# Second feed-forward, first product: seven Strassen-Winograd block products per pair of hidden tiles in place of eight, with the squared rows kept in DRAM

## The reference

```python
def rms_norm(x, gain):
    y = x * lax.rsqrt(jnp.mean(x * x, axis=-1, keepdims=True) + EPS)
    return y * gain

def sq_relu_mlp(h, w1, w2):            # w1: 1024 x 4096, w2: 4096 x 1024
    return jnp.square(jax.nn.relu(h @ w1)) @ w2
...
        h = h + sq_relu_mlp(rms_norm(h, mlp_norm_gain[layer]), mlp_w1[layer], mlp_w2[layer])
    return rms_norm(h, final_norm_gain)[:, N_META:]
```

## Time and profile before

| | us |
|---|---|
| median of three runs | 2773.19 (2771.89 to 2775.13) |
| the profiled execution | 2769.4, span 2767.6 |
| second feed-forward within it | 2028.55 to 2746.76 |

### The profile page before, as it was taken

One profiled execution on the slowest core, in us unless ns is written; L12 is line 12 of the kernel. 1 busy time (PEld: TensorE's weight loads), 2 busy tenths in 40 slices (PEclk: granted clock), 3 DMA queues, 4 the chain that ended last, 5 costly groups with the idle time before them and its releaser, 6 DMA issues.

```text
span 2767.6 us, 43631 instructions
## 1 busy us (share of the span) xinstructions
PE 2692.9 (97%) x18459; PEld 2423.2 (88%) x18459; DVE 1328.1 (48%) x1552; ACT 752.3 (27%) x1177; POOL 925.8 (33%) x403
## 2 busy tenths in 40 slices
PE   7998999999999999999999999999989999999998
PEld 7897998999999999999888888887768888888887
DVE  5387887442222322235677777779353222222234
ACT  3116886120100010002344344444221000110003
POOL 3130001344433443344323232324334444444441
PEclk9999999999999999999999999999999999999999
DMA  4110000111111111113111111112111111111111
GB/s 158 31 31 8 0 0 15 47 39 46 46 47 47 48 45 46 53 46 107 33 39 32 39 32 39 32 38 91 42 33 52 46 46 46 52 45 45 46 52 70
DMA packets 178141, 125.49 MB, mean 45 GB/s; under 512 B 4818, under 2 KB 171044, under 8 KB 177990
## 3 DMA queue, kind: packets, MB, share of 16 engines
q1 hardware_dynamic: 176694, 118.47, 14.0%
q10 hardware_dynamic: 1296, 4.73, 0.4%
HBM read 114.80 MB, written 8.39 MB: 45 GB/s over the span
## 4 chain that ended last, share of the span: by engine, by line
PE 84%; DVE 9%; issue 4%; ACT 3%; DMA 0%; ACTq 0%; SPq 0%; DVEq 0%
PE ps L1337 74%; PE ps L1471 3%; PE ps L1596 2%; PE ps L1564 1%; DVE kk L1172 1%; ACT prob L618 1%; PE ps L1421 1%; PE ps L1634 1%; ACT kk L716 1%; DVE kk L1169 1%; DVE tmp L901 1%; DVE y L967 0%; PE ps L1609 0%; DVE ssq L893 0%; DVE amax L1008 0%
## 5 line engine op out<-in xcount | busy, mean ns | idle before, releaser
L1337 PE MATMUL ps<-xh,wsp 128*128 128x512 f32 (+2 forms) x4864 | 1122.5, 355 | 13.8 <-POOL wsp L497 6.3
L495 POOL TENSOR_TENSOR wsp<-raw,ones 128x1024 fp32r<-128x1024 f32 x198 | 383.5, 1937 | 1784.8 <-PE ps L1337 1749.7
L1337 PEld LDWEIGHTS ps<-xh,wsp 128*128 128x128 f32 x4864 | 840.5, 189 | 100.3 <-issue 15.3
L1337 PE MATMUL ps<-xl,wsp 128*128 128x348 f32 (+2 forms) x2432 | 617.7, 351 | 0.0
L1337 PE MATMUL ps<-ah,wsp 128*128 128x348 f32 (+2 forms) x2560 | 567.0, 350 | 0.0
L497 POOL TENSOR_TENSOR wsp<-raw,wsp 128x1024 fp32r<-128x1024 f32 x198 | 533.5, 2694 | 15.5
L1337 PEld LDWEIGHTS ps<-ah,wsp 128*128 128x128 f32 x2560 | 443.1, 188 | 44.7
L1337 PEld LDWEIGHTS ps<-xl,wsp 128*128 128x128 f32 x2432 | 430.9, 189 | 44.3
L666 ACT ACTIVATE tmp<-tmp 128x1044 f32<-128x1044 f32 (+1 forms) x64 | 68.5, 1071 | 1096.1 <-DVE tmp L1070 555.6
L1337 PE MATMUL ps<-al,wsp 128*128 128x348 f32 (+1 forms) x1280 | 322.5, 349 | 0.0
L1337 PEld LDWEIGHTS ps<-al,wsp 128*128 128x128 f32 x1280 | 225.2, 188 | 23.2
(11 more groups left out here) (212 smaller groups left out, 2688.0 us busy)
## 6 DMA issues: line engine op xcount, KB each, us to landing
raw<-in_w SPq DMA_DIRECT2D x128, 512.0 KB, 3.7
raw<-in_c_w_in SPq DMA_DIRECT2D x40, 512.0 KB, 3.8
raw<-in_ab_w_in SPq DMA_DIRECT2D x12, 512.0 KB, 3.7
xst<-in_x SPq DMA_DIRECT2D x8, 512.0 KB, 6.6
raw<-in_ab_w_out SPq DMA_DIRECT2D x8, 512.0 KB, 3.5
h_kept<-h ACTq DMA_DIRECT2D x8, 512.0 KB, 2.6
h<-h_kept SPq DMA_DIRECT2D x8, 512.0 KB, 5.8
out<-ost SPq DMA_DIRECT2D x16, 256.0 KB, 3.0
```

What stands on the lines that cost most here:

```text
L495: nc.gpsimd.tensor_tensor(wsp[:, slot, 0, :], raw[:, slot, :], one, ALU.mult).then_inc(w_high, 1)
L1337: ins = M(ps[:, 3 * s + c, 0:n], w(a, k), b(k)[:, c0:c0 + n], start=(k == first and a == 0 and b is xa), stop=(k == last and a == 1))
```

## The change

Only the second feed-forward changes. Its first product is cut in blocks. Two hidden tiles (256 columns of w1) are a pair, `PAIRS` = 16. The inner width 1024 is halved, and so are the tokens. That is a 2 x 2 by 2 x 2 block product. `product(p, s, ...)` makes one of seven block products of pair p by the Strassen-Winograd scheme, 12 matmuls of 512 columns into one bank. So a pair takes 84 matmuls where two tiles took 96.

- **Weights.** GpSimd makes four sums of weight blocks per pair (`add` into `sw0` to `sw2`) and seven low parts (`low`), all of 512 columns. ScalarE makes the seven high parts (`high`, by a copy), each at most four products ahead (`wop` has four slots). In pairs 0 and 1 GpSimd makes these too.
- **Tokens.** At the start VectorE and ScalarE make four sums of token blocks (`ts`, `t3s`), each with high and low part for four row tiles. One replaces a quarter of `xh` and `xl`, the others are `t2h`, `t3h`, `t4h` and their low parts.
- **Results.** VectorE makes seven additions of 512 columns per pair, each from a bank and SBUF, then four rectifying steps within SBUF (`relu_half`). ScalarE copies one bank (`copy_first`), squares the four halves and stores each to the DRAM tensor `hidden_rows` (`keep`).
- **Second product.** The order is now all 16 pairs, then all eight `down` chunks. SP reloads each hidden row tile into `tmp`, ScalarE rounds it (`hidden_high`), VectorE takes the low part (`hidden_low`). `hh` and `hl` have two buffers of four tiles. `wsp` and `wop` share memory.

The diff, cut to its core (names are as in the changed kernel):

```diff
+        def bank_of(g):
+            return (2, 5, 0, 1, 3, 4)[g % 6] if g < 14 else (0, 1, 3, 4, 2, 5, 6, 7)[(g - 14) % 8]
...
+            def pair_load(p, part, free, count):
+                v1 = w1[1].rearrange("(k p) n -> p k n", p=P)
+                sp.wait_ge(free, count)
+                nc.sync.sem_inc(c_sp, 1)
+                nc.sync.dma_start(k4(raw[:, part, :]), v1[:, CH * part:CH * (part + 1), 2 * P * p:2 * P * (p + 1)]).then_inc(t_land[part], 16)
+            for p in range(1, PAIRS):
+                pair_load(p, 0, t_add, 4 * p)
+                if p == 1:
+                    pair_load(p, 1, t_low, 7)
+                else:
+                    pair_load(p, 1, t_low, 7 * p - 3)
...
+            def hidden_load(t):
+                if t == 0:
+                    sp.wait_ge(n_rc, 12)
+                elif t == 1:
+                    sp.wait_ge(t_low, 7 * PAIRS)
+                else:
+                    sp.wait_ge(l_l, 32 + t - 1)
...
+            hidden_load(0)
+            down_load(0)
+            down_load(1)
+            hidden_load(1)
+            for t in range(2, CH):
+                hidden_load(t)
+            for i in range(2, 32):
+                down_load(i)
+                if i + 2 < 32:
+                    hidden_load(i + 2)
...
+            def high(g, a):
+                if g < 2:
+                    pool.wait_ge(w_used, U_MLP1 - 1)
+                elif g < 4:
+                    pool.wait_ge(z_ready, HG_LAST + KT)
+                else:
+                    pool.wait_ge(t_done, g - 3)
+                nc.gpsimd.tensor_tensor(operand(g, 0), a, one4, ALU.mult).then_inc(t_high, 1)
+            def low(g, a):
+                pool.wait_ge(t_high, g + 1)
+                nc.gpsimd.tensor_tensor(operand(g, 1), a, operand(g, 0), ALU.subtract).then_inc(t_low, 1)
+            high(2, weight(1, 0))
+            low(2, weight(1, 0))
+            add(sw0, sw1[:], weight(0, 0), ALU.subtract)
+            pool.wait_ge(t_add, 2)
+            pool.wait_ge(n_ssq, 21)
+            add(sw2, sw0[:], weight(1, 0), ALU.subtract)
+            pool.wait_ge(t_add, 3)
+            high(3, sw2[:])
+            low(3, sw2[:])
...
+                landed(p, 0)
+                low(g, weight(0, 0))
+                landed(p, 1)
+                pool.wait_ge(t_low, 7 * p - 1)
+                add(sw1, weight(0, 1), weight(1, 1), ALU.add)
...
+                low(g + 1, sw0[:])
...
+                    high(g + 2, weight(1, 0))
+                low(g + 2, weight(1, 0))
+                pool.wait_ge(t_low, 7 * p)
+                add(sw2, sw0[:], weight(1, 0), ALU.subtract)
+                if own:
+                    high(g + 3, weight(1, 1))
...
+            def down_split(i):
+                if i < 2:
+                    pool.wait_ge(t_done, 7 * PAIRS - (1 if i == 0 else 0))
+                split(U_MLP1 + i, i % 2, 8 * (U_MLP1 + i - i % 2) + 16)
...
+            for k in range(CH):
+                act.wait_ge(z_free, HG_LAST + k + 1)
+                A(quarter(xh, k, 0), quarter(h, k, 0), ACT.Copy, scale=gain[:, k:k + 1]).then_inc(n_hi, 1)
+                A(x12[:, k, :], quarter(h, k, 1), ACT.Copy, scale=gain[:, k:k + 1]).then_inc(x_12, 1)
+                square_row(k)
+            for i in range(CH):
+                sum_high(i, quarter(xh, i, 1), ts[:, i, :])
+                act.wait_ge(z_free, HG_LAST + CH + i + 1)
+                A(xh[:, CH + i, real], h[:, CH + i, real], ACT.Copy, scale=gain[:, CH + i:CH + i + 1]).then_inc(n_hi, 1)
+                square_row(CH + i)
+            def copy_first(p):
+                act.wait_ge(t_done, 7 * p + 1)
...
+                A(p1[:], product_bank(p, 0), ACT.Copy).then_inc(t_cp, 1)
+            def high(g, a, ready, count):
+                act.wait_ge(ready, count)
+                act.wait_ge(t_done, g - 3)
+                A(operand(g, 0), a, ACT.Copy).then_inc(t_high, 1)
+                act.wait_ge(t_sq, 4 * p + n + 1)
+                nc.scalar.dma_start(hidden_rows[2 * p + b // 2][:, (b % 2) * HALF_T:(b % 2 + 1) * HALF_T], hid[b][:]).then_inc(s_hid[b], 16)
...
+                ahead(p, 3)
+                square(p - 1, 2, 3)
+                keep(p - 1, 1, 2)
+                copy_first(p)
+                ahead(p, 4)
+                square(p - 1, 3, 1)
+                keep(p - 1, 2, 3)
+                ahead(p, 5)
+                keep(p - 1, 3, 1)
+                ahead(p, 6)
+                if p == PAIRS - 1:
+                    act.wait_ge(t_done, LAST + 2)
+                    for t in range(CH):
+                        hidden_high(t)
...
+            for t in range(CH, 32):
+                if t >= 2 * CH:
+                    act.wait_ge(z_ready, E_MLP1 + 8 * (t // CH - 1))
+                hidden_high(t)
...
+            for k in range(CH):
                 add(HG_LAST + k, k % 2, k, True)
-                finish(3, k)
+                dve.wait_ge(n_hi, 24 + k + 1)
+                V.scalar_tensor_tensor(quarter(xl, k, 0), quarter(h, k, 0), gain[:, k:k + 1], quarter(xh, k, 0), ALU.mult, ALU.subtract).then_inc(x_l, 1)
+                dve.wait_ge(x_12, k + 1)
+                V.scalar_tensor_tensor(ts[:, k, :], quarter(h, k, 0), gain[:, k:k + 1], x12[:, k, :], ALU.mult, ALU.subtract).then_inc(x_s, 1)
+                if k:
+                    add_square(k)
+                add(HG_LAST + k, k % 2, k, True)
+                dve.wait_ge(x_h, i + 1)
+                V.tensor_tensor(quarter(xl, i, 1), ts[:, i, :], quarter(xh, i, 1), ALU.subtract).then_inc(x_l, 1)
+                dve.wait_ge(n_hi, 24 + k + 1)
+                V.scalar_tensor_tensor(xl[:, k, real], h[:, k, real], gain[:, k:k + 1], xh[:, k, real], ALU.mult, ALU.subtract).then_inc(x_l, 1)
+                add_square(k)
+            def sum_second(i):
+                dve.wait_ge(x_l, 5 + 2 * i)
+                V.scalar_tensor_tensor(ts[:, i, :], quarter(h, CH + i, 1), gain[:, CH + i:CH + i + 1], ts[:, i, :], ALU.mult, ALU.add).then_inc(x_s, 1)
...
+            def sum_low(n, dst, src, high):
+                dve.wait_ge(x_s, n + 1)
+                dve.wait_ge(x_h, n + 1)
+                V.tensor_tensor(dst, src, high, ALU.subtract).then_inc(x_l, 1)
...
+            sum_second(0)
+            sum_second(1)
+            second_low(0)
+            sum_second(2)
+            second_low(1)
+            sum_second(3)
+            second_low(2)
+            sum_third(0)
+            second_low(3)
+            for i in range(1, CH):
+                sum_third(i)
+                third_low(i - 1)
+            sum_fourth(0)
+            third_low(3)
+            for i in range(1, CH):
+                sum_fourth(i)
+                fourth_low(i - 1)
+            fourth_low(3)
+            dve.wait_ge(t_done, 3)
+            dve.wait_ge(t_cp, 1)
+            V.tensor_tensor(hid[0][:], p1[:], product_bank(0, 2), ALU.add).then_inc(t_rd, 1)
...
             norm(3)
-            mlp(1, E_MLP1, 4, False)
+            relu_half(0)
+            dve.wait_ge(t_rd, 6)
+            relu_half(2)
+            relu_half(3)
+            def hidden_low(t):
+                dve.wait_ge(l_h, 32 + t + 1)
+                V.tensor_tensor(hl[t // CH % 2][:, t % CH, N_META:TOK], tmp[:, t % 2, N_META:TOK], hh[t // CH % 2][:, t % CH, N_META:TOK], ALU.subtract).then_inc(l_l, 1)
+            for p in range(1, PAIRS):
+                final = p == PAIRS - 1
+                dve.wait_ge(t_done, 7 * p + 2)
+                dve.wait_ge(t_cp, p + 1)
+                V.tensor_tensor(uv[:], p1[:], product_bank(p, 1), ALU.add).then_inc(t_rd, 1)
...
+                if final:
+                    hidden_low(0)
+                else:
+                    relu_half(0)
...
+                if final:
+                    hidden_low(2)
+                    dve.wait_ge(t_done, 7 * p + 7)
+                    freed(p, 1)
+                    V.tensor_tensor(hid[1][:], uv[:], product_bank(p, 6), ALU.subtract).then_inc(t_rd, 1)
+                    hidden_low(3)
+                    relu_half(0)
...
+            for c in range(8):
+                for k in range(KT):
+                    add(E_MLP1 + 8 * c + k, k % 2, k, True)
+                    if c == 7:
+                        finish(4, k, False)
+                    elif k % 2:
+                        hidden_low(4 * (c + 1) + k // 2)
...
+            def product(p, s, high, low, ready=None):
+                g = 7 * p + s
...
+                pe.wait_ge(t_low, g + 1)
+                for k in range(CH):
+                    if ready is not None:
+                        ready(k)
+                    for side, x in ((0, high), (0, low), (1, high)):
+                        ins = M(product_bank(p, s), wop[:, g % 4, side, k * P:(k + 1) * P], x(k),
+                                start=(k == 0 and side == 0 and x is high), stop=(k == CH - 1 and side == 1))
+                ins.then_inc(t_done, 1)
...
+            product(0, 0, *b11, part_ready(1, 1))
```

(20 more changed lines are left out.)

301 lines of the change are left out of this document (286 added, 15 removed).

## The result

The changed kernel takes 2778.0 us (median of 8 runs, 2776.2 to 2784.8), the kernel before 2772.5 in the runs beside it. The medians stand 5.5 us apart, the means (2779.2 and 2772.1) 7.2. The ratio, which goes by the means, is 1.0026, 95% interval 1.0014 to 1.0037: slower by a quarter of a per cent. The profiled execution of the changed kernel took 2776.6 us, with a span of 2774.8, 7.2 more than the profiled one of before. Up to 2005 us, in code that the change leaves alone, they stand 0.82 to 0.83 later than before's.

What follows compares the result with a forecast made beforehand. TensorE, busy 97% of the span, was taken as the bound, so only its count and waits matter. Terms -44.3 + 24.0 + 18.3 + 12.6 + 4.2 = +14.8 us gave 2788.0 on the median, range 2767 to 2804.

Steps and rivals of the forecast that it cites:

- the likeliest case: Whole kernel: the forecast of 2788.0 us, nearly all slower, own range 2779 to 2798, chance 0.54.
- rival 2: Waits at chunk ends and switch: short waits leave the clock alone, without 12.6 us; time 2775.4, chance 0.13.
- The count: First product: 16 pairs lose 12 matmuls each, 192 x 0.231, so 44.3 us less.
- the steady pairs: Pairs 2 to 15: 19.4 us each, the other engines fitting within that, taken at no cost.
- Rival 3: Pairs 2 to 15: GpSimd bounds them at 20.6 us a pair, 17 us more, time 2805; chance 0.12.
- Rival 4: Matmuls into the same bank as the one before cost more, 10 ns each on 1344; time 2801, chance 0.06.
- Rival 1: Pairs 0 and 1: the start is covered, 24 VectorE steps under 21 us, costing +1.5; time 2765.5, chance 0.15.
- The chunk ends: Second product: TensorE waits 2.62 us for the fourth low part at seven ends, +18.3 us.
- The switch: From pairs to chunks: TensorE waits for tile 3's low part, +4.2 us, bounds 2 to 7.
- The start: Pairs 0 and 1: VectorE's 24 steps take turns with GpSimd, 35.8 us idle, +24.0 us; bounds +1.5 and +59.
- the free bank: Start of the stage: TensorE's first product does not wait for an accumulation; taken at 2025.5, 3.05 us earlier.
- the clock: After seven chunk ends and the switch: 3.4 us at 1.2 GHz each, 8 x 1.57, +12.6 us; lower bound 0.

Runs made afterwards that it cites:

- e4: Changed kernel with the seventh product of pairs 2 to 15 summing two of its four blocks, leaving out part of the result; 2763.7 us.
- e1: Changed kernel with VectorE making the low part of each next chunk's fourth tile after the seventh add instead of the eighth; 2756.4 us.
- e5: Changed kernel with reloads, weight splits and low parts reordered at the switch to the second product; 2777.6 us.
- e7: Changed kernel with GpSimd, after the fourth weight operand's low part, waiting until VectorE's 24 token low parts are made; 2779.2 us.
- e11: Changed kernel with the fourth tile's low part at chunk ends cut in two halves, one each side of the eighth add; 2781.7 us.
- e12: The changed kernel run once more with no edit; 2779.0 us.
- e10: Changed kernel with e1 and e5, ScalarE making early high parts, GpSimd held before pair 1's operands, and first tile's low part one add earlier; 2743.1 us.
- e13: e10 with the fourth norm's root ahead of ScalarE's waiting high parts and its broadcast two products later in pair 1; 2743.6 us.

## Why the prediction was right and wrong

**The outcome.** Slower by more than 0.2% had 0.70, and it is slower by 0.26% by the means; by the medians it is 0.20%, and the interval (0.14 to 0.37%) leaves the threshold open. The time of 2778.0 lies in the range of 2767 to 2804, but a little under the likeliest case's own range (2779 to 2798), and the shift is half of the forecast. It lies between rival 2 (short waits leave the clock alone, 2775.4) and the forecast, since three of eight waits are followed by a slow clock, not eight and not none.

**The count and the steady pairs** held: 19.46 us a pair against 19.4, and GpSimd busy 80.5 of 100 us, or 15.7 a pair, where the sum of estimates gave 15.6. Rival 3 is refuted by `e4`, since even pairs of 18.07 us are not held up. Rival 4 is refuted too: twelve matmuls in a row into one bank start 0.2317 us apart, as before's do. Rival 1 asked for 24 steps in under 21 us, and they took 33.8.

**The chunk ends** were the best step: 2.62 us at seven ends, read from the queue order and four rows, measured 2.61. `e1` shows that this step alone, with what the clock adds, is what makes the kernel slower.

**The switch** came out at 4.0 for 4.2. The forecast named the fourth tile's path, and `e5` shows that this was not all of it: with the fourth tile's reload no longer in line behind the third's, the third tile's path and the last subtraction still left 3.05 of 4.26 us.

**The start** came out as a term (22.4 for 24.0), but with luck, by errors that partly cancel. The turn-taking is shown by `e7`. Its price was too high: the step "in turns, one step passes per GpSimd instruction" charged 2.02 or 1.72 us a turn, and a turn takes 1.57. The two instructions' times must not be added in full. So the 24 steps took 33.8 us, not 38.2. On the other side, 8.7 idle us of before were 6.4, since its matmuls stand 0.2317 apart and not 0.231, which I took from a count in 100 us. The start 3.2 us sooner (forecast 3.05) is in part luck as well: the free bank gave 1.0, and another 1.0 came from before's own last matmuls ahead of the stage, which ran at a granted clock of 0.51 (2025.10 to 2028.50) while the changed kernel's ran at 1.00.

**The step that failed is the clock.** "If each chunk end and the switch below is followed by one, 8 x 1.57" was sized at 12.6 us and measured 4.7. That is nearly all of the miss of 8.2. The size of one slow stretch was right (1.5 to 1.6 us), and that such a wait can cause one was right; that each does was read into two examples. The earlier trace rows show one wait of 2.3 us and one that was longer, followed by 0.52 and 0.50, and no wait that was followed by nothing, so I gave "each" the likeliest place and named 0 as the lower bound. `e11` and `e12` show that neither the length nor the program decides alone. The honest term would have been a part of the eight, with 0 and 12.6 as bounds, and so a forecast of some 2781.

## What to carry to other kernels

When a product runs through its operands in chunks, look at the one instruction that the next chunk waits for, and at its place in its engine's queue against the last add: one place cost seven waits, 20.7 us, and the sign of the whole change. Price a TensorE wait by itself and once more by what the clock may do after it: here 2.6 us cost 3.1 on average, and 3.7 us cost 6.4, every time. Where VectorE and GpSimd both work from SBUF, count the instructions of the one that fall into the critical stretch of the other, and put them at about a microsecond each (at 512 columns); taking them away gains only as far as their own results are not wanted next, as `e7`, `e10` and `e13` each showed with another wait.

## What the hardware did that I had not expected

- Shorter waits can be followed by more low clock: 5 of 7 ends after gaps of 2.30 us, 16 of 49 after 2.84, and 7 of 7, twice as long, after 3.98.
- VectorE's `TENSOR_SCALAR` on 116 x 116, one tile input and a column, takes turns with GpSimd too: nine take 2.06 us with GpSimd idle beside all but the first, and 7.27 beside it.
- In turns of 512 columns GpSimd's own instruction grows little (1.04 to 1.30 us alone, 1.37 to 1.76 in turns), VectorE's more than doubles (0.67 to 0.75 alone, 1.52 to 1.79). VectorE bears the larger part of the price.
- The same program can take another course: in its second trace the changed kernel had 3.3 us more of a wait for the norm in pair 1, and pairs 0 and 1 took 74.2 us instead of 70.9.
